# Inverse transforms on even and odd tokens, and the sums of the spectra's products on VectorE

## What is computed

```
h = rmsnorm(x);  [q|k|v|r|g_lr|hyena] = h @ w_in
o_gla = gated linear attention in both directions (4 heads), rmsnorm, * silu(r)
u = short_conv(hyena);  v, x1, x2 = split(u)          # 512 channels each
z = x1 * fft_long_conv(v, K0);  z = x2 * fft_long_conv(z, K1);  o_hy = rmsnorm(z)
x = x + [o_gla | o_hy] @ w_out
x = x + swiglu(rmsnorm(x))

fft_long_conv(u, K):  irfft(rfft(u, 2L) * K, 2L)[:L]  (+ skip * u)
```

## Time and profile before

| | before |
|---|---|
| median of 3 runs | 1454.93 us (1453.61 to 1455.14) |
| the profiled execution, its own time | 1453.7 us |
| span of its trace | 1451.9 us |
| PE busy | 1390.1 us (96%) |
| POOL busy | 689.6 us (47%) |
| ACT busy | 484.5 us (33%) |
| DVE busy | 463.1 us (32%) |
| granted TensorE clock, mean | 0.988 |

### The profile page before, as it was taken

The page is one execution under the profiler, slowest core; times in us unless marked ns, Lnnn a source line. Parts: engine busy times, 40 slices in busy tenths (PEclk is TensorE's granted clock), DMA queues, the critical chain, the costliest instruction groups (busy, mean ns, idle before and its releaser), DMA issues.

```text
span 1451.9 us, 16432 instructions
## 1 busy us (share of the span) xinstructions
PE 1390.1 (96%) x6832; PEld 1100.7 (76%) x6832; DVE 463.1 (32%) x657; ACT 484.5 (33%) x733; POOL 689.6 (47%) x423
## 2 busy tenths in 40 slices
PE   6799999998999999999998999999989999999997
PEld 4577777787788778888866777777768888888885
DVE  5844864433102310000055676554250000000003
ACT  5734332233322222321247433322342232232112
POOL 2543653443555544544323665633625555554441
PEclk9899999999999999999999999999989999999999
DMA  7211111111433322332311211111223333333231
GB/s 258 65 42 40 36 45 59 44 58 58 139 98 91 92 83 87 116 102 88 102 58 58 59 44 59 59 31 43 87 58 96 94 102 98 91 106 108 92 100 75
DMA packets 31177, 116.82 MB, mean 80 GB/s; under 512 B 3456, under 2 KB 3584, under 8 KB 30720
## 3 DMA queue, kind: packets, MB, share of 16 engines
q1 hardware_dynamic: 31104, 115.78, 25.5%
HBM read 113.67 MB, written 2.10 MB: 80 GB/s over the span
## 4 chain that ended last, share of the span: by engine, by line
PE 84%; DVE 11%; ACT 3%; issue 1%; POOL 1%; DMA 0%; POOLq 0%; SPq 0%; DVEq 0%; ACTq 0%
PE ps L1017 16%; PE ps L1019 15%; PE ps L1018 15%; PE ps L1024 7%; PE ps L1027 7%; PE ps L1025 7%; PE ps L1218 4%; PE ps L1204 3%; PE ps L1140 2%; DVE amat L864 1%; PE ps L1085 1%; PE ps L1165 1%; DVE xs L751 1%; DVE ring L848 1%; DVE cum L828 1%
## 5 line engine op out<-in xcount | busy, mean ns | idle before, releaser
L653 POOL TENSOR_TENSOR w_lo<-w_raw,w_hi 128x1024 fp32r<-128x1024 f32 x198 | 475.2, 2401 | 522.5 <-ACT w_hi L374 522.5
L1017 PE MATMUL ps<-h_hi,w_hi 128*128 128x512 f32 x1104 | 454.0, 411 | 1.5 <-DVE h_lo L757 1.5
L1019 PE MATMUL ps<-h_hi,w_lo 128*128 128x512 f32 x1104 | 433.5, 393 | 0.0
L1018 PE MATMUL ps<-h_lo,w_hi 128*128 128x512 f32 x1104 | 433.2, 392 | 0.0
L374 ACT ACTIVATE w_hi<-w_raw 128x1024 fp32r<-128x1024 f32 x198 | 208.0, 1051 | 201.4 <-PE ps L1027 200.3
L1017 PEld LDWEIGHTS ps<-h_hi,w_hi 128*128 128x128 f32 x1104 | 209.7, 190 | 54.7 <-issue 11.8
L1018 PEld LDWEIGHTS ps<-h_lo,w_hi 128*128 128x128 f32 x1104 | 209.7, 190 | 49.4 <-issue 7.6
L1019 PEld LDWEIGHTS ps<-h_hi,w_lo 128*128 128x128 f32 x1104 | 209.2, 190 | 45.1
L993 DVE TENSOR_TENSOR hid<-ps,sg 128x512 f32<-128x512 f32 x44 | 30.4, 692 | 438.4 <-PE ps L1019 438.4
L1024 PE MATMUL ps<-w_hi,hid_hi 128*128 128x512 f32 x352 | 139.2, 396 | 1.8 <-POOL w_lo L653 1.8
L1025 PE MATMUL ps<-w_lo,hid_hi 128*128 128x512 f32 x352 | 138.8, 394 | 0.0
(11 more groups left out here) (141 smaller groups left out, 1441.5 us busy)
## 6 DMA issues: line engine op xcount, KB each, us to landing
w_raw<-in_units SPq DMA_DIRECT2D x198, 512.0 KB, 3.6
par<-in_par SPq DMA_DIRECT2D x2, 1310.5 KB, 9.0
gain<-in_gain SPq DMA_DIRECT2D x5, 512.0 KB, 4.6
x<-in_x SPq DMA_DIRECT2D x4, 512.0 KB, 7.2
out_y<-x SPq DMA_DIRECT2D x4, 512.0 KB, 2.6
cst<-in_cst SPq DMA_DIRECT2D x1, 1536.0 KB, 15.7
mask_f<-in_mask SPq DMA_DIRECT2D x1, 640.0 KB, 12.7
cst<-in_cst SPq DMA_DIRECT2D x1, 224.0 KB, 3.9
```

The source lines that it names most:

```text
L653: nc.gpsimd.tensor_tensor(w_lo[:, g % RING], w_raw[:, g % RAW], w_hi[:, g % RING].bitcast(F32), ALU.subtract).then_inc(s_lo, 1)
L1017: nc.tensor.matmul(out, hi, act_hi, start=start, stop=False)
L1018: nc.tensor.matmul(out, hi, act_lo, start=False, stop=False)
L1019: return nc.tensor.matmul(out, lo, act_hi, start=False, stop=stop)
```

## The change

The 256 frequencies of a transform with an odd grid pair up: frequency f and frequency 255-f have, at even tokens, the same cosine and opposite sign of sine, and at odd tokens the other way round. So the second group of the tables is reordered (g = 255 - f) with its sine's sign turned. The inverse then needs only the sum of the two groups' spectra for the even tokens and only their difference for the odd ones: two components in place of four, for 128 tokens each. What changes:

- VectorE forms the sums and differences itself, for every n (two instructions, as the removed `sums` on GpSimd), and after every second n the four folded spectra (two additions into `prod`, two subtractions into `spec`). It raises `folded`.
- GpSimd's `sums` is gone.
- `back` has 8 matmuls of 128 columns in place of 8 of 256, and waits for `folded`.
- `gating` reads its bank in the order even tokens, odd tokens.
- The table of the inverse is half as wide; ScalarE's `hyena_square` has one wait less.

```diff
-K_WIN = K_INV + 4 * SEQ
+K_WIN = K_INV + 4 * P
...
+        even_odd = ((prod[:, 0], prod[:, 1]), (spec[:, 0], spec[:, 1]))
...
-            def sums(L, n):
-                pool.wait_ge(prd.sem, prd.at(L, n + 1))
-                d = n % 2
-                re, im = spec[:, 2 * d], spec[:, 2 * d + 1]
-                nc.gpsimd.tensor_tensor(re, re, prod[:, 0], ALU.subtract)
-                nc.gpsimd.tensor_tensor(im, im, prod[:, 1], ALU.add).then_inc(yfd.sem, 1)
...
-                nc.vector.tensor_tensor(spec[:, 2 * d], ur, kr, ALU.mult)
+                nc.vector.tensor_tensor(re, ur, kr, ALU.mult)
                 nc.vector.tensor_tensor(prod[:, 0], ui, ki, ALU.mult)
                 nc.vector.tensor_tensor(prod[:, 1], ur, ki, ALU.mult)
-                nc.vector.tensor_tensor(spec[:, 2 * d + 1], ui, kr, ALU.mult).then_inc(prd.sem, 1)
+                nc.vector.tensor_tensor(im, ui, kr, ALU.mult).then_inc(prd.sem, 1)
+                v.wait_ge(prd.sem, prd.at(L, n + 1))
+                nc.vector.tensor_tensor(re, re, prod[:, 0], ALU.subtract)
+                nc.vector.tensor_tensor(im, im, prod[:, 1], ALU.add).then_inc(yfd.sem, 1)
+                if d:
+
+                    v.wait_ge(yfd.sem, yfd.at(L, n + 1))
+                    for c in range(2):
+                        nc.vector.tensor_tensor(even_odd[0][c], spec[:, c], spec[:, 2 + c], ALU.add)
+                    for c in range(2):
+                        last = nc.vector.tensor_tensor(even_odd[1][c], spec[:, c], spec[:, 2 + c], ALU.subtract)
+                    last.then_inc(folded.sem, 1)
...
-                pe.wait_ge(yfd.sem, yfd.at(L, 2 * i + 2))
+                pe.wait_ge(folded.sem, folded.at(L, i + 1))
...
-                    for f in range(COMPS):
-                        last = nc.tensor.matmul(ps[:, 6 + b, SEQ * c:SEQ * c + SEQ],
-                                                spec[:, f, P * (2 * b + c):P * (2 * b + c) + P], inv[:, f],
-                                                start=f == 0, stop=f == COMPS - 1)
+                    for e in range(2):
+                        for f in range(2):
+                            last = nc.tensor.matmul(ps[:, 6 + b, SEQ * c + P * e:SEQ * c + P * e + P],
+                                                    even_odd[e][f][:, P * (2 * b + c):P * (2 * b + c) + P],
+                                                    inv[:, 2 * e + f], start=f == 0, stop=f == 1)
```

More of the change, by code:

```diff
@@ L298, in build @@
         yfd = Signal(sem("s_yfd"), 8)
+        folded = Signal(sem("s_folded"), 4)
         invp = Signal(sem("s_invp"), 8)
@@ L516, in hyena_square @@
                     act.wait_ge(gated.sem, gated.at(L, 8))
-                    act.wait_ge(yfd.sem, yfd.at(L, 8))
                 nc.scalar.activation(sq[:, s], u[:, 8:12, SEQ * s:SEQ * s + SEQ], ACT.Square).then_inc(sqd.sem, 1)
@@ L697, in _ @@
                     lo_unit(L * UNITS + slot + 2)
-                    if (slot - 1, 1) in D_AT:
-                        sums(L, D_AT[slot - 1, 1])
                     exponents(L, slot)
-                    if (slot, 0) in D_AT:
-                        sums(L, D_AT[slot, 0])
                 for h in range(HEADS):
@@ L892, in products @@
                 kr, ki = kf[:, o, 2 * d], kf[:, o, 2 * d + 1]
+                re, im = spec[:, 2 * d], spec[:, 2 * d + 1]
                 v.wait_ge(ufp.sem, ufp.at(L, n + 1))
@@ L905, in gating @@
                 z = u[:, 4 * (o + 1) + 2 * b:4 * (o + 1) + 2 * b + 2, SEQ * s:SEQ * s + SEQ]
-                nc.vector.tensor_tensor(z, ps[:, 6 + b, :].rearrange("p (c t) -> p c t", c=2), z, ALU.mult)\
+                z = z.rearrange("p c (t e) -> p c t e", e=2)
+                nc.vector.tensor_tensor(z, ps[:, 6 + b, :].rearrange("p (c e t) -> p c t e", c=2, e=2), z, ALU.mult)\
                     .then_inc(gated.sem, 1)
@@ L1410, in constants @@
     f = np.arange(P)
-    dft = np.stack([np.cos(angle(f)), -np.sin(angle(f)), np.cos(angle(f + P)), -np.sin(angle(f + P))])
-    back = dft.transpose(0, 2, 1) * 2.0 / n
+    g = SEQ - 1 - f
+    dft = np.stack([np.cos(angle(f)), -np.sin(angle(f)), np.cos(angle(g)), np.sin(angle(g))])
+    back = np.stack([dft[c, e::2].T for e in range(2) for c in range(2)]) * 2.0 / n
     dft = dft.reshape(COMPS, 2, P, P).transpose(2, 0, 1, 3).reshape(P, -1)
```

## The result

The changed kernel is slower by 0.7%: 1465.07 us median of 4 runs (1463.20 to 1466.01) against 1454.79 us for the kernel before beside it (1453.61 to 1455.14). The ratio is 1.0072, 95% interval 1.0058 to 1.0085. The forecast of 1454.9 us was wrong, and the time lies above its range of 1446 to 1463 us. The profiled execution took 1463.2 us (span 1461.4 us) against 1453.7 us, so its trace has 9.5 us to explain.

What follows compares the result with a forecast made beforehand. TensorE, busy 96% of the span, was taken to bound the kernel, with VectorE ending its waits. A layer: -12.5 + 2.7 + 2.5 + 1.4 + 2.9 + 3.0 = 0.0 us, so 1454.9 us; range 1446 to 1463 us.

Steps and rivals of the forecast that it cites:

- The gain of TensorE: Long convolutions: each inverse falls from 3.45 to 1.88 us, gaining 1.57 us, 12.5 us for the 8 of a layer.
- its model, line 1165: Matmuls of the new form already in the trace: 16 instructions, 128 rows by 128 columns in float32, 1.88 us.
- The estimate of 2.6 us: Inverse priced by the skill's 81 ns spacing, two passes per instruction: 16 x 162 ns, gaining only 6.8 us a layer.
- Slots 12, 16 and 20: VectorE's sums and folds make TensorE later there: +2.7, +2.5 and +1.4 us a layer.
- Slot 22: Sums and folds precede head scaling: 1.7 us late if second scaling beats `w_lo`, else 4.1; a tie, taken as +2.9.
- The clock: TensorE's granted clock falls after the new stalls in slots 12 and 16, 1.5 us each: +3.0 us a layer (0 to 7).
- the third: Slower rival: `w_lo` first in slot 22, clock falls there too; +2.7 us a layer, 1460.3 us; chance 0.29.
- its dearer price of 2.3 us a fall: Within the slower rival of three clock falls: 2.3 us for a fall in place of 1.5, giving 1465 us.
- The rest cost nothing: Smaller table, strided `gating` read, GpSimd and ScalarE ending earlier, and ScalarE's removed wait: no cost.

## Why the prediction was wrong, point by point

- **The gain of TensorE: right, 7% small.** Forecast 1.57 us an inverse, measured 1.67; 13.4 us a layer in place of 12.5. The new inverse takes 1.78 us, its model, line 1165, gave 1.88. The estimate of 2.6 us, from the spacing that the Trainium skill gives, page TensorE: Matmul & The Clock Gate, section Back-to-back issue gap, did not hold: 16 instructions took 1.78 us. It had counted that spacing twice for each instruction, while the profile lists one weight load for each (6832 of both), so the doubling may be at fault and not the page; no run tells these apart.
- **Slots 12, 16 and 20: right.** Forecast +2.7, +2.5, +1.4; measured +2.8, +2.8, +1.4. The waits were to be 5.2 and 4.0 us long and were 5.16 and 4.09. In slot 12 the `w_lo` held the first fold and the rest took turns with GpSimd at 1.03 us (estimate 1.08), as set out. Only a wait on VectorE's own result was priced wrong, at 0.03 us and not 0.1, which is under 0.2 us in each place.
- **Slot 22: the tie was not a middle.** I saw that either `w_lo` or the second scaling goes first, at 1.7 or 4.1 us, and wrote 2.9, a value that neither course gives. `w_lo` went first, by 0.05 us, and it cost 4.0 us (2.1 + 1.9). This term was 1.1 us a layer too small. By the Trainium skill, page SBUF — State Buffer, section Who interferes with whom, the order of issue decides who blocks, and the run with the reciprocal moved agrees: 0.24 us ahead, no second wait.
- **The clock: the step that failed.** Forecast 3.0 us a layer, from one fall in the second layer of before that cost 1.5 us, taken twice. Measured 6.6 and 7.0 us. Two things were wrong. A fall after a wait of 4 to 5 us cost 1.6 to 3.0 us: the one I took the price from was among the cheapest, and its rows end at 800 us, while the clock was still 0.81 from 800 to 801 (1.7 us in all). And there were three in each layer: slot 22 has 1.85 us of waiting, 0.66 us of work and 2.10 us of waiting, which together lowered the clock too, while the single wait of 1.56 us, with the reciprocal moved, did not. Both could be read in the trace of before. Between the out-projection and the feed-forward part TensorE waits twice for the norm (here in the first layer):

```profile
362.84 0.66 PE L1035 MATMUL ps<-cst,xs 128*128 128x128 f32 x4 [2.78 <-DVE xs L751]
365.59 1.11 PE L1035 MATMUL ps<-cst,xs 128*128 128x128 f32 x4 [2.10 <-DVE xs L751]
```

and the stretches behind these waits, in the first and the second layer (columns as in the earlier trace rows), are at a lower clock:

```profile
364.00:380.00 16.00, 13.64 (x53) 11.01 (x54) 4.02 (x5) 5.55 (x7) 8.10 (x4) 0.80 0.55 186
1070.00:1090.00 20.00, 14.45 (x53) 11.14 (x52) 7.54 (x11) 9.52 (x16) 9.35 (x4) 0.74 0.28 79
```

The clock is 0.50 from 364 to 370 us and from 1074 to 1082; TensorE works in 3.6 and 5.4 us of that, so these two falls cost at least 1.8 and 2.7 us.
- **The sum.** -13.4 + 2.8 + 2.8 + 1.4 + 4.0 + 6.6 = +4.2 us (4.6 in the second layer), against 0.0. Of the miss 3.8 us are the clock's, 1.5 the waits', and 0.9 the gain gives back. The rival that held is the third, the clock falls at three stalls, with its dearer price of 2.3 us a fall (1465 us); the mean of the six falls is 2.3 us. That its 1465 us is met to 0.1 us is luck: it has +5.1 us a layer where the traces have +4.2 and +4.6. It had a chance of 0.29, and the range ended inside it. The price of a fall stands in the sum as often as the clock falls, so an error in it is multiplied by six; the range should have held this rival up to its dearer price.
- **The rest cost nothing: right.** `gating` with its strided read is as long as before (median 0.69 us), and no wait names it.

## What to carry to other kernels

Work given to an engine with a low average costs what stands behind it in that engine's list: here the sums and folds cost 11 us of waits a layer ahead of the merges and the scaling, and a few places later the layer was as short as with the halved inverses alone. Count a wait of TensorE twice where it is as long as those that lowered the clock here (3.4 us and more), once for itself and once for the clock afterwards, and look at short waits close together as one. Take the price of such a fall from all those that the trace shows, not from one. Where two courses are tied by less than the error of the sum, forecast one of them and let the range hold the other; and then make the tie go the right way, since one instruction of 0.25 us can be enough.

## What the runs showed of the hardware

- TensorE's granted clock went from 2.4 to 1.2 GHz in or just behind waits of 4.1 and 5.2 us, and stayed there while TensorE was working without a gap: it was 0.50 from 216 to 222 us and 0.87 from 222 to 224 in the kernel after. A fall cost 1.5 to 3.0 us. The same fall cost 2.1 us in one layer and 2.9 in the other (slot 12), and 3.0 and 1.6 (slot 16).
- The traces show two things behind that spread. One is how much of the lower clock falls into the wait itself: in slot 12 the clock is 0.62 from 164 to 166 us in the first layer, with the wait ending at 166.84; in the second it is still 0.82 from 880 to 882, with the wait ending at 881.94. The other is how long it stays low: behind the wait of slot 16 until past 222 us in the first layer (wait ended at 216.18), until just short of 936 in the second (ended at 932.13). What decides either stays open; no run was made for it.
- Throwaway matmuls of TensorE during its waits prevented all six of these falls: 13.7 us of 1465, at no cost that can be seen in the stretches. The falls elsewhere in the kernel, such as those of the earlier trace rows, remained.
- A fold of 512 columns on VectorE and GpSimd's instruction of 256 columns take turns, one of each in 1.03 us, and a wait of VectorE on its own last result costs some 0.1 us (0.71 us between starts in place of 0.61).
